# Two transformer blocks in one launch: 32 more projections read the input's two parts as one 512-column operand

## What is computed

```
# first block
a   = silu(rms_norm(causal_conv(a_val * sigmoid(a_gate))))      # 31 taps a channel
y_a = a @ w_conv_out                                            # "co": 8 tiles of 128 outputs
y_b = attention(...) @ w_attn_out                               # "ao": 8 tiles
x   = x + (sigmoid(gate_a) * y_a + sigmoid(gate_b) * y_b) @ w_out   # "wo": 8 tiles
x   = x + ffn(x)
# second block
z   = rms_norm(x) @ w_in_2              # gate_a, gate_b of it are "g2": 16 tiles
mix = sigmoid(gate_a) * (mla(...) @ mla_w_o) + sigmoid(gate_b) * (gla(...) @ gla_w_o)
x   = x + mix @ w_out_2;  x = x + ffn_2(x)
```

## Time and profile before

| | us |
|---|---|
| median of three runs | 841.23 (839.57 to 841.70) |
| the profiled execution | 839.11 |
| its span, first to last instruction | 837.3 |
| TensorE busy | 827.0 (99%) |
| VectorE busy | 648.4 (77%) |
| ScalarE busy | 554.2 (66%) |
| GpSimd busy | 231.0 (28%) |
| "ao" jobs | from 195.8 to 219.15 |
| "co" jobs | from 219.15 to 242.19 |
| "g2" jobs and the attention between them | from 535.6 to 594.5 |

### The profile page before, as it was taken

One profiled execution on the slowest core, in us unless ns is written; L12 is line 12 of the kernel. 1 busy time (PEld: TensorE's weight loads), 2 busy tenths in 40 slices (PEclk: granted clock), 3 DMA queues, 4 the chain that ended last, 5 costly groups with the idle time before them and its releaser, 6 DMA issues.

```text
span 837.3 us, 16575 instructions
## 1 busy us (share of the span) xinstructions
PE 827.0 (99%) x6006; PEld 772.1 (92%) x6006; DVE 648.4 (77%) x1170; ACT 554.2 (66%) x1020; POOL 231.0 (28%) x245
## 2 busy tenths in 40 slices
PE   9999999999999999999999999999999999999996
PEld 9998999999999999999889988999998988888885
DVE  7997979997979998787766868847589866666552
ACT  8877999986756776665545775476657665655451
POOL 0387853332311243433101000020022332222110
PEclk9999999999999999999999999999999999999998
DMA  7766554546565476555646454435346566665641
GB/s 274 222 201 177 178 181 127 164 137 198 162 193 176 134 222 199 180 182 169 232 157 216 152 176 130 148 128 177 110 148 196 178 206 196 183 194 176 227 126 51
DMA packets 43168, 146.12 MB, mean 175 GB/s; under 512 B 4928, under 2 KB 7504, under 8 KB 43088
## 3 DMA queue, kind: packets, MB, share of 16 engines
q1 hardware_dynamic: 42192, 144.13, 54.9%
q10 hardware_dynamic: 896, 0.94, 0.4%
HBM read 144.00 MB, written 1.05 MB: 173 GB/s over the span
## 4 chain that ended last, share of the span: by engine, by line
PE 92%; ACT 4%; DVE 2%; issue 1%; DMA 1%; DVEq 0%; POOL 0%; ACTq 0%; SPq 0%; POOLq 0%
PE px L547 21%; PE px L551 17%; PE px L553 16%; PE px L552 16%; PE px L548 11%; ACT whi L918 1%; PE px L558 1%; PE px L559 1%; PE px L557 1%; PE px L645 1%; PE px L624 1%; DVE wlo L1426 1%; PE px L636 1%; PE px L773 1%; DMA raw<-ws 1%
## 5 line engine op out<-in xcount | busy, mean ns | idle before, releaser
L1426 DVE TENSOR_TENSOR wlo<-raw,whi 128x1024 fp32r<-128x1024 f32 x265 | 330.4, 1253 | 29.2 <-ACT whi L918 29.2
L918 ACT ACTIVATE whi<-raw 128x1024 fp32r<-128x1024 f32 x265 | 278.1, 1052 | 56.0 <-PE px L548 27.3
L551 PE MATMUL px<-hx,whi 128*128 128x256 f32 x1024 | 296.3, 289 | 0.3 <-DVE hx L1443 0.3
L553 PE MATMUL px<-hx,wlo 128*128 128x256 f32 x1024 | 289.8, 283 | 0.0
L552 PE MATMUL px<-hx,whi 128*128 128x256 f32 x1024 | 289.7, 283 | 0.0
L551 PEld LDWEIGHTS px<-hx,whi 128*128 128x128 f32 x1024 | 196.2, 192 | 3.6 <-issue 1.2
L552 PEld LDWEIGHTS px<-hx,whi 128*128 128x128 f32 x1024 | 196.3, 192 | 0.5
L553 PEld LDWEIGHTS px<-hx,wlo 128*128 128x128 f32 x1024 | 196.2, 192 | 0.0
L2064 POOL TENSOR_TENSOR CA<-CA,ct 128x256 f32<-128x256 f32 x90 | 92.8, 1031 | 94.6 <-DVE wlo L1426 74.6
L547 PE MATMUL px<-fx,whi 128*128 128x512 f32 x330 | 115.7, 393 | 0.0
L547 PE MATMUL px<-hx,whi 128*128 128x512 f32 x320 | 111.2, 392 | 0.0
(11 more groups left out here) (322 smaller groups left out, 1319.6 us busy)
## 6 DMA issues: line engine op xcount, KB each, us to landing
raw<-ws SPq DMA_DIRECT2D x265, 512.0 KB, 3.6
tb<-tabs SPq DMA_DIRECT2D x16, 128.0 KB, 3.4
X<-xs SPq DMA_DIRECT2D x4, 256.0 KB, 3.8
raw<-ws SPq DMA_DIRECT2D x3, 256.0 KB, 5.1
out<-X SPq DMA_DIRECT2D x3, 256.0 KB, 2.2
vc<-vecs SPq DMA_DIRECT2D x1, 315.5 KB, 6.3
raw<-ws ACTq DMA_DIRECT2D x1, 256.0 KB, 3.8
msk<-lmask ACTq DMA_DIRECT2D x1, 256.0 KB, 2.9
```

Source lines behind the costliest of these rows:

```text
L551: e.matmul(b[:, 0:S], H, xh, start=first, stop=False)
L553: m = e.matmul(b[:, 0:S], L, xh, start=False, stop=end)
L918: e.activation(whi[:, n % NSL, :], raw[:, n % NRAW, :], ACT.Copy).then_inc(s_hi, 1)
L1426: e.tensor_tensor(wlo[:, n % NSL, :], raw[:, n % NRAW, :], whi[:, n % NSL, :], ALU.subtract).then_inc(s_lo, 1)
```

## The change

The "ao", "co" and "g2" jobs join `WIDE`. Each of the 32 then leaves two half sums, so the reader changes. For "ao" and "co" ScalarE copies the first half from PSUM into one of three buffers `tb` (`first_half`), VectorE adds the second half to it (`whole_row`, which frees the bank), and then gates from that buffer (`gated_row`). For "g2" ScalarE copies the first half into the gate's tile, VectorE adds the second half (`whole_gate`, one job later in its order), and ScalarE takes the tanh in place (`tanh2`, one job later in its order). `mix2` is what `mix` did for the second block.

```diff
 WIDE = ({("dn", i) for i in range(KD)} | {("fd", i) for i in range(KD - 1)} | {("wo", i) for i in range(KD)} |
-        {("wo2", i) for i in range(KD)} | {(k, i) for k in ("fg", "fu") for i in range(2, FT)})
+        {(k, i) for k in ("ao", "co", "wo2") for i in range(KD)} | {(k, i) for k in ("fg", "fu") for i in range(2, FT)} |
+        {("g2", i) for i in range(16)})
...
 # ScalarE
+            def first_half(key, n):
+                e.wait_ge(s_mm, ENDS[key])
+                if n >= 3:
+                    e.wait_ge(s_og1, n - 2)
+                e.activation(tb[:, n % 3, :], px_of[key, 0][:, 0:S], ACT.Copy).then_inc(s_oc, 1)
...
                     e.activation(sg[:, n % 3, :], CA[:, n, :], ACT.Tanh, scale=cg5[:, n:n + 1]).then_inc(s_ctanh, 1)
+                first_half(("ao", i), i)
...
             for i in range(KD):
                 beside(("co", i))
+                first_half(("co", i), KD + i)
                 split_high(0, i, GA, ax[:, i, 0, :], ENDS["ao", 7])
...
+            def tanh2(n):
+                e.wait_ge(*BANK[("g2", n), 0])
+                e.activation(gate2(n), gate2(n), ACT.Tanh, scale=0.5).then_inc(s_gt, 1)
...
                     e.wait_ge(s_mm, ENDS[key])
-                    e.activation(G[:, n % 8, :], px_of[key, 0][:, 0:S], ACT.Tanh, scale=0.5).then_inc(BANK[key, 0][0], 1)
+                    e.activation(gate2(n), px_of[key, 0][:, 0:S], ACT.Copy).then_inc(s_gc, 1)
+                    if n:
+                        tanh2(n - 1)
                     linear(key)
+                elif key == ("go", 1):
+                    tanh2(15)
...
 # VectorE
+            def whole_row(key, n):
+                e.wait_ge(s_oc, n + 1)
+                t = tb[:, n % 3, :]
+                e.tensor_tensor(t, t, px_of[key, 0][:, S:2 * S], ALU.add).then_inc(BANK[key, 0][0], 1)
+            def gated_row(G, i, n):
+                e.wait_ge(*BANK[(("ao", "co")[n // KD], i), 0])
+                e.scalar_tensor_tensor(out=G[:, i, :], in0=G[:, i, :], scalar=1.0, in1=tb[:, n % 3, :], op0=ALU.add,
+                                       op1=ALU.mult).then_inc(s_og1, 1)
...
-                e.wait_ge(s_mm, ENDS["ao", i])
+                whole_row(("ao", i), i)
                 e.wait_ge(*BANK[("g", 8 + i), 0])
-                e.scalar_tensor_tensor(out=GB[:, i, :], in0=GB[:, i, :], scalar=1.0, in1=px_of[("ao", i), 0][:, 0:S],
-                                       op0=ALU.add, op1=ALU.mult).then_inc(BANK[("ao", i), 0][0], 1)
+                gated_row(GB, i, i)
...
             for i in range(KD):
                 beside(("co", i))
+                whole_row(("co", i), KD + i)
...
-                mix(0, ("co", i), i, GA, GB, ("ao", i))
+                gated_row(GA, i, KD + i)
+                mix(i)
...
+            def whole_gate(n):
+                e.wait_ge(s_gc, n + 1)
+                e.tensor_tensor(gate2(n), gate2(n), px_of[("g2", n), 0][:, S:2 * S], ALU.add).then_inc(
+                    BANK[("g2", n), 0][0], 1)
             def late(key):
                 beside(key)
                 if key[0] == "g2":
+                    if key[1]:
+                        whole_gate(key[1] - 1)
                     linear(key)
                 else:
                     i = key[1]
+                    if i == 0:
+                        whole_gate(15)
                     e.wait_ge(s_mm, ENDS[key])
-                    e.wait_ge(*BANK[("g2", 8 + i), 0])
+                    e.wait_ge(s_gt, 9 + i)
```

More of the change, by code:

```diff
@@ L436, in two_blocks @@
             "s_rot", "s_sin", "s_glr", "s_rk", "s_dl", "s_da", "s_ds"))
+        s_gc, s_gt = sem("s_gc"), sem("s_gt")
         s_pad = sem("s_pad")
@@ L445, in two_blocks @@
         s_cor = sem("s_cor")
+        s_oc, s_ow, s_og1 = sem("s_oc"), sem("s_ow"), sem("s_og1")
         s_og, s_ov = sem("s_og"), sem("s_ov")
@@ L490, in two_blocks, with gate2 @@
         posi = ug[:, 4, :].bitcast(I32)
+        def gate2(n):
+            return (GA2 if n < 8 else GB2)[:, n % 8, :]
         def row_done(f, n):
@@ L1376, in late @@
                     n = key[1]
-                    G = GA2 if n < 8 else GB2
                     e.wait_ge(s_mm, ENDS[key])
-                    e.activation(G[:, n % 8, :], px_of[key, 0][:, 0:S], ACT.Tanh, scale=0.5).then_inc(BANK[key, 0][0], 1)
+                    e.activation(gate2(n), px_of[key, 0][:, 0:S], ACT.Copy).then_inc(s_gc, 1)
+                    if n:
+                        tanh2(n - 1)
                     linear(key)
+                elif key == ("go", 1):
+                    tanh2(15)
             for n in range(7):
@@ L1630, in _, with mix, mix2 @@
                     lows(ahead(last_chunk(("ao", i))) + 1)
-                e.wait_ge(s_mm, ENDS["ao", i])
+                whole_row(("ao", i), i)
                 e.wait_ge(*BANK[("g", 8 + i), 0])
-                e.scalar_tensor_tensor(out=GB[:, i, :], in0=GB[:, i, :], scalar=1.0, in1=px_of[("ao", i), 0][:, 0:S],
-                                       op0=ALU.add, op1=ALU.mult).then_inc(BANK[("ao", i), 0][0], 1)
+                gated_row(GB, i, i)
                 if i == 0:
                     taps(CONV_END + 1)
-            def mix(a, key, i, GA_, GB_, other):
+            def mix(i):
+                e.wait_ge(s_og1, KD + i + 1)
+                e.scalar_tensor_tensor(out=GA[:, i, :], in0=GA[:, i, :], scalar=0.5, in1=GB[:, i, :], op0=ALU.mult,
+                                       op1=ALU.add).then_inc(s_mix[0], 1)
+            def mix2(i):
+                key = ("mo", i)
                 e.wait_ge(s_mm, ENDS[key])
-                e.scalar_tensor_tensor(out=GA_[:, i, :], in0=GA_[:, i, :], scalar=1.0, in1=px_of[key, 0][:, 0:S],
+                e.scalar_tensor_tensor(out=GA2[:, i, :], in0=GA2[:, i, :], scalar=1.0, in1=px_of[key, 0][:, 0:S],
                                        op0=ALU.add, op1=ALU.mult).then_inc(BANK[key, 0][0], 1)
                 e.wait_ge(*BANK[key, 0])
[L1644 to L1650, removed]
+                e.wait_ge(*BANK[("go", i), 0])
+                e.scalar_tensor_tensor(out=GA2[:, i, :], in0=GB2[:, i, :], scalar=0.5, in1=GA2[:, i, :], op0=ALU.mult,
+                                       op1=ALU.add).then_inc(s_mix[1], 1)
             def mix_low(a, i, G, to, hi):
@@ L2010, in _ @@
                     beside(("mo", i))
-                e.wait_ge(*BANK[("g2", i), 0])
-                mix(1, ("mo", i), i, GA2, GB2, ("go", i))
+                e.wait_ge(s_gt, i + 1)
+                mix2(i)
                 if i > MIX_G:
```

## The result

| | median, us | runs |
|---|---|---|
| before | 840.80 (839.57 to 841.70) | 4 |
| changed | 852.60 (851.68 to 854.29) | 4 |

The medians are 11.8 us apart. The ratio, which is worked out over the runs and is not the quotient of the two medians, is 1.0145, 95% interval 1.0129 to 1.0162, or 10.8 to 13.6 us slower. The profiled execution of the changed kernel took 854.29 us, the slowest of its four, with a span of 852.4 us; that of before 839.11 us with 837.3.

The account below looks back on a forecast made before the run. TensorE, busy 827.0 of 837.3 us, was taken to bound the kernel. Stalls with savings 10.7, clock 0.5 and lag 0.3, less 1.7 for "g2", made 9.8 us more: 841.2 + 9.8 = 851.0 us, range 845.5 to 857.

Parts of the forecast that it names:

- What bounds, and TensorE's gain: Whole kernel: TensorE's own steps bound it; the wide form in "ao", "co" and "g2" saves 2.8 us together.
- the term of the gate jobs: "g2" jobs: the wide form saves 0.0133 us on each of 128 input tiles, 1.7 us.
- The hand-over in "ao": "ao": ScalarE and VectorE work in turn, making `conv_low` late; TensorE stalls 7.5 us in ("co", 0), 5 to 10.
- The ring in "co": "co": copy, add, gate, mix, split, high part take 3.04 us against TensorE's 2.77; stall 4.3 us at ("wo", 0).
- My side remark: At ("wo", 0): without the backlog from "ao", the stall would be 2.4 us.
- The rival built on that remark: "co": only its round of hand-overs binds, without backlog from "ao"; 840.8 us, no change; chance 5%.
- The clock: TensorE's pauses in ("co", 0) and ("wo", 0): the clock may fall to half; 0.5 us taken.
- the second pause: In ("wo", 0), behind the last mixes: 1 and 3 us; a clock fall only there costs up to 3.3 us.
- The gate jobs as a cover: "g2": 1.07 us of cover before the four squares absorbs the added work; price 0, up to 0.5 us once.
- The sum: Whole kernel: 10.7 + 0.5 + 0.3 - 1.7 = 9.8 us more, giving 851.0 us.
- the 0.3 for lag: First FFN behind the "wo" jobs: VectorE's lag may pass on, between 0 and 0.42 us; 0.3 taken.
- The rival that both engines absorb the copies: "ao" and "co": idle ScalarE and VectorE cover the copies, TensorE's 2.8 us come through; 838.4 us; chance 5%.

Follow-up runs that it names:

- e4: Kernel before with the 32 jobs wide and nothing else, readers taking the first half alone (second halves left out): 839.18 us, ratio 0.9972.
- e2: Changed kernel with ScalarE's `split_high` of each "co" job moved one job later, behind the next job's copy: 850.22 us, ratio 1.0102 to before.
- e3: Changed kernel with both moves, the "ao" copy ahead of the tanhs and `split_high` one job later: 842.58 us, ratio 1.0011 to before.
- e8: Changed kernel with "ao" and the last "co" job narrow as before, and `split_high` one job later: 837.50 us, ratio 0.9972 to before.
- e1: Changed kernel with ScalarE's "ao" copy moved ahead of the high parts and tanhs of its index: 847.85 us, ratio 1.0081 to before.
- e10: Changed kernel with "ao" narrow and read as before, "co" and gate jobs as in the change: 845.22 us, ratio 1.0067 to before.
- e9: Changed kernel with unread matmuls in TensorE's pauses (20 and 10, then 7 and 11) to keep the clock up: 849.73 us, ratio 1.0128 to before.
- e6: Kernel before with the change in "ao" and "co" alone, gate jobs as before: 854.22 us, ratio 1.0169.
- e7: Changed kernel with more unread matmuls in TensorE's pauses (40 and 16, then 8 and 22): 857.59 us, ratio 1.0206 to before.
- e5: Kernel before with the change in the second block's 16 gate jobs alone: 838.60 us, ratio 0.9986.

## Why the prediction was right, step by step

- **What bounds, and TensorE's gain.** Right in kind: e4 shows 2.4 us (interval 1.2 to 3.5) for the 2.8. Mis-sized is the term of the gate jobs, 1.7 us given, 1.05 in the trace: jobs 2 to 6 gained 0.1 us each as said, but the nine that stand between the softmax attention's float32 matmuls went from 2.95 to 2.90 us, half the gain. Their price had been read from one gate job that stands elsewhere. The "co" tiles were 0.3467 us apart in e2, e3 and e8 and 0.353 in the profiled executions of the change and of e1.
- **The hand-over in "ao".** Right, and close: `first_half(4)` predicted for 216.05, seen at 216.70; `first_half(5)` 222.0 and 222.75; `conv_low` 3-5 224.4 and 225.15; and 0.5 us of each difference is this execution's later start. TensorE idled 6.1 us, and ("co", 0) took 8.3 us longer where 7.5 were given; the 0.75 us are the half clock on its last two tiles. e1 shows it is the order of the copy.
- **The ring in "co".** Right: 3.12 us against 3.04 (add to gate took 0.53 and not 0.45). The last mix ended at 256.0 against 254.4: 0.5 us of that is the later start, 0.55 the seven rounds, and the rest the first mix. e2 and e10 show the ring. My side remark that without the backlog the stall would be 2.4 us was wrong; e10 has 3.6 us of idle time, and its ("wo", 0) took 7.48 us for 2.77. The rival built on that remark (no change) had its price too low.
- **The clock.** Here the sum was too small: I took 0.5 us, and ("wo", 1) alone lost 1.6. The first fall came, and cost nothing by the end, as I had argued (e9). I then argued that it would shrink the second pause enough to keep the clock up. It did shrink it (2.4 us of idle time where a stall of 4.3 was given), and the clock fell all the same, 1.0 us after TensorE had resumed. The Trainium skill ("TensorE: Matmul & The Clock Gate", section "HAM oscillation — how this bites in real kernels") describes a kernel whose waits between stretches of matmuls make each next stretch start at the half clock. The trace agrees for the first pause (4.6 us idle, then 0.64 us a tile). The second differs: TensorE resumed at full clock and lost it afterwards, and in e6 a pause of 2.3 us cost no clock at all. My price for a stretch at half clock came from TensorE's first 32 matmuls (6.53 us, 0.204 us each), beside which the profile reads a clock of 1.00; the same instruction took 0.114 us in e7 (80 in 9.09 us), so they were near half speed, whatever the reading says.
- **The gate jobs as a cover.** Right: e5 has no new wait of TensorE there, and neither has the changed kernel. There the four squares are done at 563.94 and wanted at 564.60, so of the 1.07 us of cover 0.66 are left:

```profile
562.61 1.33 ACT L1352 ACTIVATE sq<-go 128x256 f32<-128x256 f32 x4
...
564.60 1.89 PE L835 MATMUL px<-sq,ones 128*128 128x256 f32 x8
```

- **The sum.** In the profiled pair the stalls with their savings are 12.0 us (8.3 + 1.2 + 2.8 - 0.3) where I gave 10.7. The clock is 1.6 more and not 0.5, the gates give 1.05 and not 1.7, and nothing is seen of the 0.3 for lag: 12.0 + 1.6 - 1.05 = 12.6 us from the change, where the forecast was 9.8. The three large terms all erred towards too little, by 1.3, 1.1 and 0.65 us. The medians, 11.8 apart with an interval of 10.8 to 13.6, agree with 12.6. The mechanism was foreseen, and the size was 2 to 3 us short in 12.

The rival that both engines absorb the copies fell because idle time that is spent waiting for the other engine isn't room: from 204.5 to 219.15 VectorE was busy 8.6 us (11.4 before) and ScalarE 9.6 (12.0 before), less than before, and both later. In e3 the same added work stands in another order and costs 1 us in place of 11.8.

## What to carry to other kernels

When a result takes a detour over a second engine, look first at what stands ahead of it in that engine's written order, and follow the ring: copy, add, gate, mix, split, next copy. If a round is longer than the producer's step, it is paid at the next point where everything must be there, however idle both engines look. Taking the result of the previous round at that point (e2, e8) takes away the ring and costs no instruction. It makes the last result a little later (0.4 us of idle time at ("wo", 0) in e2 and e3), and leaving the last job in the old form (e8) took that away for 0.1 us of TensorE's time.

## What the runs showed of the hardware

- The same wide jobs on the same tile ran in one of two paces for a long stretch, 0.3467 or 0.353 us a tile, from one execution to the next, also where the kernel does not differ: the second FFN's 38 jobs, 2.0 us in all. The profiled executions of before, e1, e3, e5, e6, e8, e9 and e10 had the fast one there, those of the changed kernel, e2, e4 and e7 the slow one. The kernel before, in the 19 runs beside e1 to e4, has three from 839.2 to 839.9 and the others from 841.2 up, which is the same distance; that the two groups are the two paces is likely and not shown, and what chooses the pace stays open. A gain of 1 us needs many runs beside this.
- A float32 matmul of 128 columns, which is two instructions in the profile, took 0.23 us at full clock (e7, forty in 9.09 us), so forty of them are no light way to keep TensorE busy.
- The clock read 0.50 for 10.2 us from within the first pause on, and for 3.4 us from 1.0 us after the second; in e6 a pause of the second kind (2.3 us idle) passed without a fall.
